# Five convolution taps on ScalarE and adding DMAs, queries and keys turned: one decoder layer on one core

## The chip, the core and the metric

The kernel runs on 1 core of one Trainium2 chip. The metric is the device time of one execution in microseconds (us). The engines are called as the profile calls them: PE (TensorE), DVE (VectorE), ACT (ScalarE), POOL (GpSimd) and SP (SyncE, which issues the loads of the weights).

## What is computed

One decoder layer on 256 tokens of width 1024, all in float32: RMSNorm, one projection to 4608 columns, causal attention of 8 heads beside a convolution module, both gated and merged, an output projection, a residual, a squared-ReLU MLP and a last RMSNorm.

```python
h = rmsnorm(x, g_mix[l])
proj = h @ w_in[l]
q, k, v = the first three blocks of 512 columns, 8 heads of 64
u = proj[..., c_v:c_u] + b_glu[l]
gate_a = jax.nn.sigmoid(proj[..., c_u:c_ga])
gate_c = jax.nn.sigmoid(proj[..., c_ga:])
branch_a = moba_attention(q, k, v) @ w_attn_up[l]      # 256 tokens: plain causal attention
z = a * sigmoid(g)                                      # a, g: the halves of u
z = causal depthwise convolution of z, 31 taps, + b_dw; layernorm; silu
branch_c = z @ w_conv_pw[l] + b_conv_pw[l]
x = x + (gate_a * branch_a + gate_c * branch_c) @ w_out[l]
h = rmsnorm(x, g_ffn[l])
x = x + jnp.square(jax.nn.relu(h @ w_ff1[l])) @ w_ff2[l]
return rmsnorm(x, g_final)
```

## The kernel before, in words

Every float32 product is made of three: each weight and each activation is split into a high part in float32r and the low rest (`w_hi`, `w_lo`, `a_hi`, `a_lo`), and PE sums low by high, high by high and high by low. The weights come in units of 1 MB (512 rows by 512 columns) that SP loads into four slots of `raw`. For each unit n, ACT makes `w_hi` (`high`, L405) and DVE makes `w_lo` (`low`, L674), both three units ahead of PE; the order of work on each engine is written out by hand as one loop over n, with blocks that run at a given n.

Block b is units 2b and 2b+1. Blocks 0 and 1 are the input of the GLU, block 2 the queries (Q), 3 the keys (K), 4 the values (V), 5 to 8 the gates (GA is 5, GC is 7). Units 18 and 19 are the attention's projection, 20 and 21 the convolution's, 22 to 25 the output projection, and the rest is the MLP. A usual unit (`unit`, L980) holds tokens as the stationary operand and streams the weights in 512 columns: 24 matmuls into two PSUM banks, tokens on the partitions. ACT copies a finished block out and scales each token by its `rstd` (`take`, L448). The queries are computed turned (`queries`, L1111): weights stationary, tokens streamed in 256 columns, 48 matmuls a unit, channels on the partitions. The keys are computed as a usual block, copied to `nat`, transposed by PE after unit 8 (L1150, `S_KT`) and copied to `qk_t` (L471). The scores after units 9 to 12 (`scores`, L1067) need `k_made` and `q_made`; each pair of heads then passes over DVE (`row_max`), ACT (`exps`, `normalise`), PE (`probs_transposed`), ACT (`probs_out`) and PE (`values`). Queries keep no `rstd` in `qk_t`; it comes in as the scale of the exponential.

The convolution runs channels on the partitions: `z` holds the input with 30 columns of padding. ACT makes tap 0 with the bias (L539), and DVE adds the other 30 taps for 4 groups of channels, 120 instructions of 256 columns (L730, `conv_products`), spread over the steps by `CONV_AT` and put behind `low` in each step, except in step 15 (`S_OLO`), where the taps come ahead of `low(18)` and of the subtraction that makes `b_lo` (L871). After unit 16 (`S_LN`) PE waits for the last tap (L1168) and transposes `conv` for the LayerNorm; DVE then takes the statistics (L784).

```python
                if n == S_OLO:
                    conv_products(n)
                if n and n + AHEAD < U_LOOP + AHEAD_LOOP:
                    low(n + AHEAD)
```

Of the kernel before, what the change touches and what calls it, by code (L numbers as in the profile page):

```python
# [6 lines left out]
P = 128  # L7
T = 256
# [40 lines left out]
S_QSCALE, S_KT = 6, 8  # L49
# [3 lines left out]
S_GATE = 14  # L53
S_LN = 16
# [5 lines left out]
CONV += [(tap, c) for tap in range(10, TAPS) for c in range(4)]  # L60
CONV_AT = {2: 6, 3: 12, 4: 9, 5: 9, 6: 9, 7: 7, 8: 6, 9: 5, 10: 8, 11: 11, 12: 12, 13: 11, 14: 10, 15: 5}
assert len(CONV) == sum(CONV_AT.values()) == (TAPS - 1) * 4

# [25 lines left out]
def build(nc, x, g_mix, w_in, b_glu, w_dw, b_dw, ln_g, ln_b, w_conv_pw, b_conv_pw,  # L89
# [35 lines left out]
    with ExitStack() as ctx:  # L125
# [12 lines left out]
        a_hi = sb("a_hi", [P, KD, T], F32R)  # L138
        a_lo = sb("a_lo", [P, KD, T], F32R)
# [5 lines left out]
        v_nat = sb("v_nat", [P, TT, A])  # L145
        qk_t = sb("qk_t", [P, 2, CC, T])
# [33 lines left out]
        bias_bc = gfin_bc  # L180
        hid = nat[:, 0, :].rearrange("p (c t) -> p c t", c=4)
# [66 lines left out]
        conv_step = sem("conv_step")  # L248
        conv_tr = sem("conv_tr")
# [7 lines left out]
        cz_lo = sem("cz_lo")  # L257
        q_made = sem("q_made")
        q_scaled = sem("q_scaled")
        k_tr = sem("k_tr")  # L260
# [105 lines left out]
        def _(pool):  # L366
# [21 lines left out]

            inverse_root(1, ln_var[:], 2)
# [3 lines left out]
        def _(act):  # L393
# [47 lines left out]
            def queries_out():  # L441

                act.wait_ge(used, 2 * Q + 2)
                for half in range(2):
                    bank = Q_BANKS[2 * half]
                    nc.scalar.copy(qk_t[:, 0, 2 * half:2 * half + 2], ps[:, bank:bank + 2, 0:T]).then_inc(q_made, 1)

            def take(b):  # L448
# [59 lines left out]

            def set_bias(col):
# [6 lines left out]
            for n in range(U_LOOP):  # L516
# [43 lines left out]
                if n == S_GATE:  # L560
                    act.wait_ge(evac, GA)
# [108 lines left out]
        def _(dve):  # L670
# [76 lines left out]

            def inverse(p):
# [10 lines left out]
            for n in range(U_LOOP):  # L759
# [52 lines left out]
                if n in (U_ATTN, U_ATTN + 1):  # L812
# [3 lines left out]
                    dve.wait_ge(evac, len(ORDER) - 1)  # L816
# [39 lines left out]
                if n == U_FF:  # L856
# [3 lines left out]
                    nc.vector.reciprocal(rsq[:], ms[:, 1]).then_inc(rsq_made, 1)  # L860
                if n == S_OLO:
# [94 lines left out]
        def _(pe):  # L956
# [355 lines left out]
```

## Time and profile before

| | us |
|---|---|
| median of 3 runs | 351.67 |
| lowest and highest run | 351.25, 351.74 |
| span of the profiled execution | 350.3 |
| PE busy | 344.2 (98%) |
| DVE busy | 251.5 (72%) |
| ACT busy | 192.1 (55%) |
| PE's granted clock, mean | 0.997 |

The span runs from the first to the last instruction; the median lies 1.4 us above it. A row of a timeline gives the start, the time from start to end, and how many like instructions were merged. Neighbouring instructions overlap at their ends, so what one costs in a stream is the distance between starts. Line numbers are those of the kernel before.

### The profile page before, as it was taken

To read this page: it belongs to the slowest core of one execution; us is meant where nothing else is said; L and a number is where in the kernel's file an instruction comes from. 1 tells how busy PE (TensorE), PEld (TensorE's weight loads), DVE (VectorE), ACT (ScalarE), POOL (GpSimd) and SP (SyncE) were. 2 spreads that over 40 slices of the span, in tenths; PEclk is the share of its full clock that TensorE was granted. 3 is DMA by queue.
4 is the path that set the end of the run, shared out by engine and by line. 5 is a ranking of instruction groups with operands and counts; after the bars stand their busy time and mean duration, and the time that the engine had idled before them with its cause. 6 is when DMAs were issued, how large, how long until landed. Compare 5 with 4: busy or idle time off the path is not lost.

```text
span 350.3 us, 4670 instructions
## 1 busy us (share of the span) xinstructions
PE 344.2 (98%) x1766; PEld 289.5 (83%) x1766; DVE 251.5 (72%) x313; ACT 192.1 (55%) x236; POOL 3.5 (1%) x13
## 2 busy tenths in 40 slices
PE   8999999999999999999999999999999999999994
PEld 5889988787778888888888888888888888889884
DVE  2969999899999889965666946639466394563813
ACT  4985644698796358434674535515355163551534
POOL 1000000000000000000000000000000000000000
PEclk9999999999999999999999999999999999999998
DMA  8999455534353365783647472944729537260003
GB/s 278 349 387 377 155 206 156 206 122 153 121 198 130 120 239 156 265 254 110 198 157 227 152 252 90 299 180 128 248 102 301 178 121 243 115 239 0 0 0 120
DMA packets 34429, 64.23 MB, mean 183 GB/s; under 512 B 1360, under 2 KB 6000, under 8 KB 34416
## 3 DMA queue, kind: packets, MB, share of 16 engines
q1 hardware_dynamic: 34056, 63.56, 54.0%
q10 hardware_dynamic: 360, 0.49, 0.4%
q8 instruction: 9, 0.15, 0.2%
q14 instruction: 4, 0.03, 0.0%
HBM read 63.00 MB, written 1.05 MB: 183 GB/s over the span
## 4 chain that ended last, share of the span: by engine, by line
PE 98%; DVE 0%; issue 0%; DVEq 0%; ACT 0%
PE ps L971 20%; PE ps L972 19%; PE ps L973 19%; PE ps L1230 17%; PE ps L1238 9%; PE ps L958 4%; PE ps L1018 2%; PE ps L1122 1%; PE ps L1121 1%; PE ps L1123 1%; PE ps L1029 1%; PE ps L1072 1%; PE ps L1097 1%; PE ps L998 1%; PE ps L1191 0%; PE ps L1282 0%
## 5 line engine op out<-in xcount | busy, mean ns | idle before, releaser
L971 PE MATMUL ps<-w_hi,a_lo 128*128 128x512 f32 x256 | 100.9, 394 | 0.0
L972 PE MATMUL ps<-w_hi,a_hi 128*128 128x512 f32 x256 | 99.8, 390 | 0.0
L973 PE MATMUL ps<-w_lo,a_hi 128*128 128x512 f32 x256 | 99.7, 390 | 0.0
L899 DVE TENSOR_TENSOR w_lo<-raw,w_hi 128x2048 fp32r<-128x2048 f32 x28 | 63.5, 2287 | 6.2 <-ACT w_hi L623 6.2
L405 ACT CAST w_hi<-raw 128x2048 fp32r<-128x2048 f32 (+1 forms) x30 | 53.7, 1799 | 19.9 <-PE ps L973 19.7
L1230 PE MATMUL ps<-b_both,w_hi 128*128 128x512 f32 x256 | 61.3, 390 | 0.0
L674 DVE TENSOR_TENSOR w_lo<-raw,w_hi 128x2048 fp32r<-128x2048 f32 x26 | 59.3, 2285 | 1.7 <-ACT w_hi L405 1.7
L623 ACT CAST w_hi<-raw 128x2048 fp32r<-128x2048 f32 x28 | 52.8, 1914 | 7.5 <-PE ps L973 7.5
L971 PEld LDWEIGHTS ps<-w_hi,a_lo 128*128 128x128 f32 x256 | 48.1, 188 | 10.1 <-issue 0.5
L973 PEld LDWEIGHTS ps<-w_lo,a_hi 128*128 128x128 f32 x256 | 48.0, 188 | 10.2
L972 PEld LDWEIGHTS ps<-w_hi,a_hi 128*128 128x128 f32 x256 | 48.1, 188 | 9.4
L1230 PEld LDWEIGHTS ps<-b_both,w_hi 128*128 128x128 f32 x256 | 47.3, 188 | 9.4
L730 DVE SCALAR_TENSOR_TENSOR conv<-z,dw,conv 128x256 f32<-128x256 f32 x120 | 48.5, 478 | 0.0
L878 DVE TENSOR_TENSOR nat<-ps,nat 128x512 f32<-128x512 f32 x16 | 11.1, 692 | 40.6 <-ACT nat L601 40.6
L601 ACT COPY nat<-ps 128x512 f32<-128x512 f32 x16 | 9.4, 587 | 52.9 <-PE ps L1238 52.8
L1238 PEld LDWEIGHTS ps<-b_both,w_lo 128*128 128x128 f32 x256 | 33.0, 191 | 1.3
L1238 PE MATMUL ps<-b_both,w_lo 128*128 128x256 f32 x256 | 33.4, 283 | 0.0
L607 ACT CAST a_hi<-nat 128x1024 fp32r<-128x1024 f32 x7 | 7.3, 1050 | 21.8 <-PE ps L973 21.6
L891 DVE TENSOR_TENSOR a_lo<-nat,a_hi 128x1024 fp32r<-128x1024 f32 x7 | 8.6, 1225 | 14.1 <-ACT a_hi L607 14.1
L971 PE MATMUL ps<-w_hi,b_both 128*128 128x512 f32 x44 | 17.3, 393 | 0.0
L973 PE MATMUL ps<-w_lo,b_both 128*128 128x512 f32 x44 | 17.1, 389 | 0.0
L972 PE MATMUL ps<-w_hi,b_both 128*128 128x512 f32 x44 | 17.1, 389 | 0.0
(138 smaller groups left out, 302.5 us busy)
## 6 DMA issues: line engine op xcount, KB each, us to landing
raw<-in_w_ff_dram SPq DMA_DIRECT2D x32, 1024.0 KB, 5.4
raw<-in_w_in_dram SPq DMA_DIRECT2D x14, 1024.0 KB, 5.9
raw<-in_w_out_dram SPq DMA_DIRECT2D x4, 1024.0 KB, 5.3
raw<-in_w_in_dram SPq DMA_DIRECT2D x14, 256.0 KB, 5.7
raw<-in_w_attn_up_dram SPq DMA_DIRECT2D x2, 1024.0 KB, 5.2
raw<-in_w_conv_pw_dram SPq DMA_DIRECT2D x2, 1024.0 KB, 5.1
res<-in_x_dram SPq DMA_DIRECT2D x2, 512.0 KB, 3.9
raw<-in_w_in_dram SPq DMA_DIRECT2D x4, 128.0 KB, 4.1
```

Source lines behind the costliest of these rows:

```text
L405: nc.scalar.copy(w_hi[:, n % SLOTS, part], raw[:, n % SLOTS, part]).then_inc(hi_made, 1)
L623: nc.scalar.copy(w_hi[:, slot], raw[:, slot]).then_inc(hi_made, 1)
L674: nc.vector.tensor_tensor(w_lo[:, n % SLOTS], raw[:, n % SLOTS], w_hi[:, n % SLOTS].bitcast(F32), ALU.subtract).then_inc(lo_made, 1)
L730: nc.vector.scalar_tensor_tensor(out=conv[:, c], in0=z[:, c, tap:tap + T], scalar=dw[:, w:w + 1], in1=conv[:, c], op0=ALU.mult, op1=ALU.ad ...
L878: nc.vector.tensor_tensor(hid[:, pair], ps[:, TB + 2 * half:TB + 2 * half + 2, 0:T], hid[:, pair], ALU.add).then_inc(sum_made, 1)
L899: nc.vector.tensor_tensor(w_lo[:, slot], raw[:, slot], w_hi[:, slot].bitcast(F32), ALU.subtract).then_inc(lo_made, 1)
L958: return nc.tensor.transpose(dst, src, ident[0:src.shape[0], 0:src.shape[0]])
L971: nc.tensor.matmul(dst, lo[:, tok], w_hi[:, slot, k], start=start, stop=False, skip_group_check=seeded)
L972: nc.tensor.matmul(dst, hi[:, tok], w_hi[:, slot, k], start=False, stop=False, skip_group_check=seeded)
L973: return nc.tensor.matmul(dst, hi[:, tok], w_lo[:, slot, k], start=False, stop=stop, skip_group_check=seeded)
L1230: nc.tensor.matmul(ps[:, TB + c], w_hi[:, slot, k, cols], b_both[:, kk].rearrange("p a t -> p (a t)"), start=kk == 0, stop=False)
L1238: last = nc.tensor.matmul(ps[:, TB + c, 0:T], w_lo[:, slot, k, cols], b_hi[:, kk], start=False, stop=kk == KD - 1)
```

## The change

The queries' function becomes `turned`, for queries and keys. For each group of 128 channels it first streams both halves of the activations (`a_both`, low and high side by side, 512 columns) under each of four `w_hi`, then `a_hi` alone (256 columns) under four `w_lo`. So the product of the low half lands in columns 256 to 511 of a bank; ACT copies that half to `qk_t` and DVE adds the other (`queries_sum` in step 6, `keys_sum` in step 8). The keys' transposes, their `take` and the copy after them go. Keys must still be scaled per token, which now lies along the columns: PE transposes `rstd` after unit 3 into a row, ACT copies it out, and DVE multiplies the keys by it. Scores and unit 10 wait for both halves of the keys.

Taps 26 to 30 leave DVE. ACT multiplies each in steps 5 to 8 (4 instructions of 256 columns a tap): the first into `conv_part` (the room of `zn`), the others by turns into two halves of `gates[:, 1]`; a DMA issued by POOL adds each of these four to `conv_part`, one after the other. In step 16 DVE waits for the last DMA and adds `conv_part` to `conv` in one instruction; PE's transposes wait for that.

```diff
-S_QSCALE, S_KT = 6, 8
+S_QSCALE, S_QSUM, S_KSUM = 6, 6, 8
+K_BANKS = (2, 3, 6, 7)
+S_ROW = 3
...
 S_GATE = 14
+S_PART = 16
...
-CONV += [(tap, c) for tap in range(10, TAPS) for c in range(4)]
-CONV_AT = {2: 6, 3: 12, 4: 9, 5: 9, 6: 9, 7: 7, 8: 6, 9: 5, 10: 8, 11: 11, 12: 12, 13: 11, 14: 10, 15: 5}
-assert len(CONV) == sum(CONV_AT.values()) == (TAPS - 1) * 4
+TAPS_ACT = {5: (26,), 6: (27,), 7: (28, 29), 8: (30,)}
+TAPS_DVE = TAPS - sum(len(taps) for taps in TAPS_ACT.values())
+CONV += [(tap, c) for tap in range(10, TAPS_DVE) for c in range(4)]
+CONV_AT = {2: 6, 3: 12, 4: 9, 5: 9, 6: 6, 7: 7, 8: 2, 9: 3, 10: 6, 11: 9, 12: 10, 13: 9, 14: 7, 15: 5}
+assert len(CONV) == sum(CONV_AT.values()) == (TAPS_DVE - 1) * 4
...
-        a_hi = sb("a_hi", [P, KD, T], F32R)
-        a_lo = sb("a_lo", [P, KD, T], F32R)
+        a_both = sb("a_both", [P, KD, 2, T], F32R)
+        a_hi, a_lo = a_both[:, :, 0], a_both[:, :, 1]
...
+        rstd_row = sb("rstd_row", [P, T])
...
+        tap_out = (gates[:, 1, 0].rearrange("p (c t) -> p c t", c=CC), gates[:, 1, 1].rearrange("p (c t) -> p c t", c=CC))
+        conv_part = zn[:].rearrange("p t c -> p (t c)").rearrange("p (c t) -> p c t", c=CC)
...
+            pool.wait_ge(part_first, CC)
+            for i in range(1, TAPS - TAPS_DVE):
+                pool.wait_ge(tap_made, CC * i)
+                if i > 1:
+                    pool.wait_ge(tap_added, 16 * (i - 1))
+                nc.gpsimd.dma_start(conv_part, tap_out[i % 2], accum_op=ALU.add).then_inc(tap_added, 16)
...
-                    nc.scalar.copy(qk_t[:, 0, 2 * half:2 * half + 2], ps[:, bank:bank + 2, 0:T]).then_inc(q_made, 1)
+                    nc.scalar.copy(qk_t[:, 0, 2 * half:2 * half + 2], ps[:, bank:bank + 2, T:2 * T]).then_inc(q_cross, 1)
...
@@ -451,12 +474,12 @@
                 act.wait_ge(used, 2 * b + 2)
                 if b == 0:
                     act.wait_ge(rstd_made, 1)
-                if b == K:
-                    act.wait_ge(glu_tr, CC)
+                if b == GC:
+                    act.wait_ge(tap_added, 16 * (TAPS - TAPS_DVE - 1))
                 if b == GA:
                     dst, fn = gates[:, 0, :, 0:W], ACT.Copy
-                elif b < 2 or b == K:
-                    dst, fn = nat[:, :, (b % 2) * W:(b % 2) * W + W], ACT.Copy
+                elif b < 2:
+                    dst, fn = nat[:, :, b * W:b * W + W], ACT.Copy
...
             def keys_out():
-                act.wait_ge(k_tr, 1)
-                nc.scalar.copy(qk_t[:, 1], chunks(SB0)).then_inc(k_made, 1)
+
+                act.wait_ge(used, 2 * K + 2)
+                for half in range(2):
+                    bank = K_BANKS[2 * half]
+                    nc.scalar.copy(qk_t[:, 1, 2 * half:2 * half + 2], ps[:, bank:bank + 2, T:2 * T]).then_inc(k_cross, 1)
...
+                for tap in TAPS_ACT.get(step, ()):
+                    act.wait_ge(z_made, CC)
+                    i = tap - TAPS_DVE
+                    if i > 2:
+                        act.wait_ge(tap_added, 16 * (i - 2))
+                    for c in range(CC):
+                        w = tap * CC + c
+                        dst = tap_out[i % 2][:, c] if i else conv_part[:, c]
+                        nc.scalar.activation(dst, z[:, c, tap:tap + T], ACT.Copy,
+                                             scale=dw[:, w:w + 1]).then_inc(tap_made if i else part_first, 1)
...
-                if n == S_KT:
+                tap_products(n)
+                if n == S_ROW:
+                    act.wait_ge(row_tr, 1)
+                    nc.scalar.copy(rstd_row[:], ps[:, SB0, 0:T]).then_inc(row_made, 1)
+                if n == 2 * K + 1:
                     keys_out()
-                if n == 2 * Q + 1:
+                elif n == 2 * Q + 1:
                     queries_out()
                 elif n < U_ATTN and n % 2 == 1 and 0 < n // 2 < GA:
                     take(n // 2)
...
-                    act.wait_ge(evac, GA)
+                    act.wait_ge(evac, GA - 1)
...
+                for half in range(2):
+                    bank = Q_BANKS[2 * half]
+                    dve.wait_ge(q_cross, half + 1)
+                    part = qk_t[:, 0, 2 * half:2 * half + 2]
+                    nc.vector.tensor_tensor(part, ps[:, bank:bank + 2, 0:T], part, ALU.add).then_inc(q_made, 1)
+
+            def keys_sum():
+
+                dve.wait_ge(row_made, 1)
+                row = rstd_row[:].rearrange("p (c t) -> p c t", c=1).to_broadcast([P, 2, T])
+                for half in range(2):
+                    bank = K_BANKS[2 * half]
+                    dve.wait_ge(k_cross, half + 1)
+                    part = qk_t[:, 1, 2 * half:2 * half + 2]
+                    nc.vector.tensor_tensor(part, ps[:, bank:bank + 2, 0:T], part, ALU.add).then_inc(k_sum, 1)
+                for half in range(2):
+                    dve.wait_ge(k_sum, half + 1)
+                    part = qk_t[:, 1, 2 * half:2 * half + 2]
+                    nc.vector.tensor_tensor(part, part, row, ALU.mult).then_inc(k_made, 1)
...
+                if n == S_PART:
+                    dve.wait_ge(tap_added, 16 * (TAPS - TAPS_DVE - 1))
+                    dve.wait_ge(conv_step, (TAPS_DVE - 1) * CC)
+                    nc.vector.tensor_tensor(conv[:], conv[:], conv_part, ALU.add).then_inc(conv_made, 1)
...
-                    dve.wait_ge(evac, len(ORDER) - 1)
+                    dve.wait_ge(evac, len(ORDER) - 2)
...
+                if n == S_QSUM:
+                    queries_sum()
+                if n == S_KSUM:
+                    keys_sum()
...
+                if hb == 1:
+                    pe.wait_ge(row_made, 1)
...
-            def queries(n):
+            def turned(n, banks):
 
                 weights(n)
                 for c in range(CC):
                     if n == 2 * Q and c == 2:
                         pe.wait_ge(z_made, 2)
+                    if n == 2 * K and c == 2:
+                        pe.wait_ge(z_made, CC)
                     cols = slice(c * P, c * P + P)
                     for k in range(HK):
                         kk = HK * (n % 2) + k
-                        dst = ps[:, Q_BANKS[c], 0:T]
-                        nc.tensor.matmul(dst, w_hi[:, n % SLOTS, k, cols], a_lo[:, kk], start=kk == 0, stop=False)
-                        nc.tensor.matmul(dst, w_hi[:, n % SLOTS, k, cols], a_hi[:, kk], start=False, stop=False)
-                        last = nc.tensor.matmul(dst, w_lo[:, n % SLOTS, k, cols], a_hi[:, kk], start=False,
-                                                stop=kk == KD - 1)
+                        nc.tensor.matmul(ps[:, banks[c]], w_hi[:, n % SLOTS, k, cols],
+                                         a_both[:, kk].rearrange("p a t -> p (a t)"), start=kk == 0, stop=False)
+                    for k in range(HK):
+                        kk = HK * (n % 2) + k
+                        last = nc.tensor.matmul(ps[:, banks[c], 0:T], w_lo[:, n % SLOTS, k, cols], a_hi[:, kk],
+                                                start=False, stop=kk == KD - 1)
                     if n == 2 * Q and c == 1:
                         glu_transposed(GLU_AT[n])
                 last.then_inc(used, 1)
...
-                if half == 0 and b >= 2:
-                    pe.wait_ge(evac, b - 1 if b <= V - 1 else b - 2)
+                if half == 0 and b in (Q, K):
+                    pe.wait_ge(evac, b - 1)
+                if n == 2 * GA:
+                    pe.wait_ge(k_made, 2)
+                if half == 0 and b > GA:
+                    pe.wait_ge(evac, b - 3)
                 if n == 2 * V:
                     pe.wait_ge(q_made, 2)
...
-                if b == Q:
-                    queries(n)
+                if b in (Q, K):
+                    turned(n, Q_BANKS if b == Q else K_BANKS)
...
-                if n == S_KT:
-                    pe.wait_ge(evac, K)
-                    pe.wait_ge(z_made, CC)
-                    transpose_chunks(SB0, lambda t, c: nat[:, t, W + c * P:W + c * P + P]).then_inc(k_tr, 1)
+                if n == S_ROW:
+                    pe.wait_ge(rstd_made, 1)
+                    pe.wait_ge(vec_made, 1)
+                    for t in range(TT):
+                        last = transpose(ps[:, SB0, t * P:t * P + P], rstd[:, 0, t:t + 1].to_broadcast([P, P]))
+                    last.then_inc(row_tr, 1)
                 if n == S_ATT:
-                    pe.wait_ge(k_made, 1)
+                    pe.wait_ge(k_made, 2)
...
                 if n == S_ATT + 2:
-                    pe.wait_ge(evac, V)
...
-                    pe.wait_ge(conv_step, (TAPS - 1) * CC)
+                    pe.wait_ge(conv_made, 1)
...
-                pe.wait_ge(evac, len(ORDER) - 2 + col)
+                pe.wait_ge(evac, len(ORDER) - 3 + col)
```

## Rows read from the trace of the kernel before

**Rows 1.** The page: busy time of each engine; the chain that ended last, by engine

```profile
PE 344.2 (98%) x1766; PEld 289.5 (83%) x1766; DVE 251.5 (72%) x313; ACT 192.1 (55%) x236; POOL 3.5 (1%) x13
PE 98%; DVE 0%; issue 0%; DVEq 0%; ACT 0%
```

**Rows 2.** Who waited for whom, PE: in total, times, longest, us

```profile
PE ps L998 <- DVE zero_b L677: 1.2, 1, 1.2
```

**Rows 3.** Timeline of PE, units 4 to 9: start us, us, engine, line, operation

```profile
30.78 0.28 PE L1121 MATMUL ps<-a_lo,w_hi 128*128 128x256 f32 x1
...
33.65 1.03 PE L958 MATMUL ps<-ident,nat 128*128 128x128 f32 x8
...
43.15 0.40 PE L971 MATMUL ps<-w_hi,a_lo 128*128 128x512 f32 x1
...
59.51 1.03 PE L958 MATMUL ps<-ident,nat 128*128 128x128 f32 x8
60.30 0.48 PE L971 MATMUL ps<-w_hi,a_lo 128*128 128x512 f32 x1
...
65.92 0.92 PE L1072 MATMUL ps<-qk_t 64*128 64x256 f32 x8
```

**Rows 4.** Timeline of PE, the first products of the MLP

```profile
177.34 2.00 PE L1230 MATMUL ps<-b_both,w_hi 128*128 128x512 f32 x8
179.18 1.12 PE L1238 MATMUL ps<-b_both,w_lo 128*128 128x256 f32 x8
180.13 3.82 PE L1230 MATMUL ps<-b_both,w_hi 128*128 128x512 f32 x16
```

**Rows 5.** Timeline of DVE from step 8 up to the LayerNorm

```profile
61.39 2.29 DVE L674 TENSOR_TENSOR w_lo<-raw,w_hi 128x2048 fp32r<-128x2048 f32 x1
...
66.95 0.70 DVE L738 TENSOR_TENSOR ps<-ps,mask 128x512 f32<-128x512 f32 x1 [0.89 <-issue]
...
89.67 0.69 DVE L738 TENSOR_TENSOR ps<-ps,mask 128x512 f32<-128x512 f32 x1
...
93.86 4.81 DVE L730 SCALAR_TENSOR_TENSOR conv<-z,dw,conv 128x256 f32<-128x256 f32 x12
...
107.35 6.02 DVE L730 SCALAR_TENSOR_TENSOR conv<-z,dw,conv 128x256 f32<-128x256 f32 x15
113.29 2.28 DVE L674 TENSOR_TENSOR w_lo<-raw,w_hi 128x2048 fp32r<-128x2048 f32 x1
115.50 1.21 DVE L871 TENSOR_TENSOR b_both<-o_t,b_both 128x1024 fp32r<-128x1024 f32 x1
116.63 1.29 DVE L784 BATCH_NORM_STATS2 stats<-ps 128x6 f32<-128x512 f32 x2
```

**Rows 6.** Timeline of DVE, two products of 512 columns out of PSUM

```profile
130.59 1.28 DVE L819 TENSOR_TENSOR nat<-ps,gates 128x512 f32<-128x512 f32 x2
```

**Rows 7.** Timeline of ACT, steps 7 to 13

```profile
54.26 1.27 ACT L466 ACTIVATE nat<-ps,rstd 128x512 f32<-128x512 f32 x2 [3.47 <-PE ps L973]
...
71.27 0.91 ACT L491 ACTIVATE probs<-probs,rinv 128x256 f32<-128x256 f32 x2 [0.24 <-DVE rinv L750]
72.08 0.68 ACT L494 ACTIVATE probs<-probs,rinv 128x128 f32<-128x128 f32 x2
...
91.66 0.57 ACT L477 ACTIVATE probs<-ps,nbias,q_scale 128x256 f32<-128x256 f32 x1 [0.57 <-DVE nbias L746]
...
96.53 1.90 ACT L405 CAST w_hi<-raw 128x2048 fp32r<-128x2048 f32 x1
```

**Rows 8.** Timeline of PE, the last scores and the transposes of conv

```profile
88.52 0.92 PE L1072 MATMUL ps<-qk_t 64*128 64x256 f32 x8
...
114.68 1.03 PE L958 MATMUL ps<-ident,conv 128*128 128x128 f32 x8
```

**Rows 9.** DMA issues by size: KB each, median us from issue to landing

```profile
res<-in_x_dram SPq DMA_DIRECT2D x2, 512.0 KB, 3.9
...
gfin_bc<-in_b_conv_pw_dram SPq DMA_DIRECT2D x1, 512.0 KB, 8.1
```

More of the change, by code:

```diff
@@ L248, in build @@
         conv_step = sem("conv_step")
+        part_first = sem("part_first")
+        tap_made = sem("tap_made")
+        tap_added = sem("tap_added")
+        conv_made = sem("conv_made")
         conv_tr = sem("conv_tr")
@@ L257, in build @@
         cz_lo = sem("cz_lo")
+        q_cross = sem("q_cross")
         q_made = sem("q_made")
         q_scaled = sem("q_scaled")
-        k_tr = sem("k_tr")
+        row_tr = sem("row_tr")
+        row_made = sem("row_made")
+        k_cross = sem("k_cross")
+        k_sum = sem("k_sum")
         k_made = sem("k_made")
@@ L507, in probs_out, with tap_products @@
                 nc.scalar.copy(probs_t[:], ps[:, TB:TB + 2, :].rearrange("p b n -> p (b n)")[:, 0:768]).then_inc(pt_made, 1)
+            def tap_products(step):
+                for tap in TAPS_ACT.get(step, ()):
[8 more added lines that the diff above has]
+                                             scale=dw[:, w:w + 1]).then_inc(tap_made if i else part_first, 1)
             def set_bias(col):
@@ L746, in row_max, with queries_sum @@
                 nc.vector.tensor_tensor(nbias[:, p], smax[:, p], q_neg[:], ALU.mult).then_inc(nbias_made, 1)
+            def queries_sum():
+                for half in range(2):
[15 more added lines that the diff above has]
+                    nc.vector.tensor_tensor(part, part, row, ALU.mult).then_inc(k_made, 1)
             def inverse(p):
@@ L1146, in _ @@
                     transpose(ps[:, SB0 + 1, P:P + TAPS * CC], dw_rows).then_inc(dw_tr, 1)
-                if n == S_KT:
-                    pe.wait_ge(evac, K)
-                    pe.wait_ge(z_made, CC)
-                    transpose_chunks(SB0, lambda t, c: nat[:, t, W + c * P:W + c * P + P]).then_inc(k_tr, 1)
+                if n == S_ROW:
[4 more added lines that the diff above has]
+                    last.then_inc(row_tr, 1)
                 if n == S_ATT:
-                    pe.wait_ge(k_made, 1)
+                    pe.wait_ge(k_made, 2)
                     pe.wait_ge(q_made, 2)
                 if n == S_ATT + 2:
-                    pe.wait_ge(evac, V)
+                    pe.wait_ge(evac, V - 1)
                 if n == S_ATT + PAIRS - 1:
```

## The prediction

> **What bounds the kernel.** I read the page first: PE is busy for 98% of the span, and the chain that ended last is PE throughout [rows 1]. Then the waits of PE: the only one is 1.2 us, before its first instruction [rows 2]. So PE never waits for data once it has begun, and DVE and ACT matter only where they come late for it. Two questions follow: what does the change do to the length of PE's own stream, and does one of the new waits of PE end later than PE arrives? For the second I laid the timelines of DVE, ACT and PE side by side between 30 and 117 us. DVE is nearly without a gap there: it is behind PE, and catches up only where the next thing it needs isn't ready. The sum is made against the span of 350.3 us, and the difference is put on the median of 351.67 us.
>
> **PE's own stream.** *Queries.* Units 4 and 5 run from 30.78 to 43.15 with eight transposes between them [rows 3]. Eight transposes cost 59.51 to 60.30 and a slower restart of 0.09 (unit 9 behind them takes 5.62 us, 60.30 to 65.92, of which 0.08 is the like change to the scores), 0.88 us together. So a unit of 48 matmuls costs (12.37 - 0.88) / 2 = 5.74 us. A usual unit costs (59.51 - 43.15) / 3 = 5.45 us [rows 3]. The columns streamed are the same in all forms, 12,288 a unit; only the cost per instruction differs.
> The new form has its like in the MLP [rows 4]: 8 matmuls of 512 columns take 179.18 - 177.34 = 1.84 us, and 8 of 256 take 0.95 us. At the usual unit's 0.227 a matmul the first would be 1.82, so each change from narrow to wide costs about 0.02 us. `turned` has four groups of 4 wide and 4 narrow: 4 x (0.91 + 0.02 + 0.475) = 5.63 us a unit; with a dearer change (0.04) 5.7, and with none 5.55. I take 5.64.
> Queries: 2 x (5.64 - 5.74) = -0.2 us. Keys: 2 x (5.64 - 5.45) = +0.4 us. *The keys' transposes* go: -0.88. *The transposes of rstd* come: two at 0.1 and a restart of 0.09, +0.3. Sum: -0.2 + 0.4 - 0.9 + 0.3 = -0.4 us, between -0.7 and -0.2. Where nothing waits, this would be all that the change is worth: the taps that DVE loses cost PE nothing before.
>
> **New waits of PE that are met.** The row: `rstd` is long made when unit 3 ends; ACT copies it while PE is in unit 4, ahead of the transposes at 33.65 by more than 1 us: nothing. The queries' banks: ACT copies the half at about 43.5, and DVE adds in step 6, at about 50.7 (two steps before 61.39), two instructions of 0.6 (1.28 for two with the tail [rows 6]); unit 8 asks at 54.9. The keys: unit 7 ends at 43.15 + 2 x 5.45 = 54.05, + 0.6 (row, queries and keys so far); ACT copies two pairs, about 1 us, in place of the `take` at 54.26 [rows 7]. DVE comes to step 8 at 61.4 as before [rows 5], since in step 6 the sums (1.2) replace three taps (1.2). Its four instructions of 512 columns cost 2.4 us; keys are ready at 63.9, and the scores ask at 65.92 - 0.4 = 65.5 [rows 3]. Met, by 1.6 us. Step 8 has 4 taps fewer (1.6 us), so DVE reaches the first `row_max` at 66.9, where before, after an idle 0.89 us, it began at 66.95 behind the scores [rows 5]: the first exponentials begin as before. The first normalisation ends at 72.76 [rows 7], and PE wants it 0.85 us of scores after unit 10, at 73.32 - 0.4 = 72.9. Met by 0.1 to 0.2 us; if PE gains 0.7 it waits here for the rest.
>
> **ACT and the adding DMAs.** Twenty products at 0.41 to 0.5 us (two of 256 columns in SBUF take 0.91 with the tail [rows 7]) are 8 to 10 us; 1.2 us of copies go. In steps 5 to 8 ACT stands idle some 15 us, the 3.47 us ahead of 54.26 among them [rows 7], so the products fit. What is queued behind them: `high` of the next step and the copies of keys and V. The trace has no adding DMA. The bounds of one of 512 KB are the nearest rows of that size, 3.9 and 8.1 us [rows 9]; it reads two sources, so I take 5.5. A tap of step 6 is multiplied at about 48.1; added by 53.6, it lets tap 29 begin 0.8 us late; the second DMA ends at 59.1 and tap 30, `high(12)` (1.9) and then V (wanted at 65.6) follow in time. The condition for no loss is two DMAs in 62.1 - 48.1 = 14 us, 7 us each. The loads of the weights are half of the DMA engines' time and land long before ACT wants them, so they pay nothing.
> Here a rule of the Trainium skill speaks against the change, in DMA: Bandwidth & Descriptors, "Anatomy of one DMA — SWDGE (gpsimd) path": a DMA issued by GpSimd costs about 2.0 us and its bytes at 436 GB/s. By it 512 KB would be 3.2 us (an estimate from that page), and with the second read that Collectives: The Full Stack, "The bandwidth ceiling", describes for the inline add, 4.4 us; no run shown so far has such a DMA.
>
> **The wait that is not met: the sum before the LayerNorm.** Before, the last tap ended at 113.3 [rows 5] and PE asked at 114.68 [rows 8]: 1.4 us to spare. Now DVE makes its last tap, then `low(18)`, then `b_lo`, and only then the add of `conv_part`; these are 2.2 + 1.1 + 1.2 us (113.29, 115.50, 116.63; the add has the shape of `b_lo`, both operands in SBUF) = 4.5 us behind the last tap [rows 5]. What DVE gains before it: 20 taps at 5.94 / 15 = 0.396 us are 7.9 us, less 1.2 and 2.4 for the sums: 4.3 us. That would leave PE just served. But part of the gain goes into waits, for DVE now runs ahead of what feeds it. Forward from the last scores:
> They start at 88.52 - 0.4 and take 0.92 [rows 8]: `row_max(3)` starts at 89.1, not 89.67; DVE, with six taps fewer in steps 9 to 11, is free 0.5 us earlier and waits. From it to the taps of step 12 it is 93.86 - 89.67 = 4.2 us: 93.3. Ten taps: 97.2. `low(16)` needs `high(16)`, which ACT makes after the last exponentials; these start 0.6 us earlier than 91.66, so `high(16)` ends at 96.53 + 1.90 - 0.6 = 97.8 [rows 7]. DVE waits 0.6 us more. Then `low(16)` 2.2, nine taps 3.6, `low(17)` 2.2, twelve taps 4.75: 110.6. Then 2.2 + 1.1 + 1.2 = 115.1. PE arrives at 114.68 - 0.4 = 114.3 and starts, after a wake-up of under 0.1, at 115.2, 0.5 us later than before. It waits 0.8 to 0.9 us.
> Afterwards nothing gives this back. PE is bound again, and the LayerNorm, the zn transposes and the SiLU hang on PE's transposes, so they shift with it; DVE takes its statistics at 116.3, when before it came only at 116.63.
>
> **Forecast.** +0.5 us: 351.67 + 0.5 = 352.2. Its own range is -0.1 to +1.3 (DVE 0.6 us earlier or 0.8 later over 25 us of dense work): 351.6 to 353.0.
>
> **Rivals.** *A, PE is served* (faster side): DVE loses none of its gain in the two waits, ends the add by 114.3, and the whole is PE's own stream, -0.4: 351.3; with the best figures, -0.7, 351.0. For it: 4.3 gained and 1.4 to spare against 4.5 needed. Against it: `high(16)` stands in front. *B, the adding DMAs are slow* (slower side): at 8.1 us each the second ends at 64.3. Tap 30 (1.65) and `high(12)` (1.9) put V at 67.9, the copy, and the table load of the exponential end at 70.4, 1.45 us later than before; PE waits 1.2 us for the first normalisation, `high(16)` comes later by about as much, and the wait at the sum stays: +1.7, 353.4. At 10 us each it is about +5. It decides from 7 us. *C, the sum is dearer or DVE is later*: the add waits for DVE alone, so every 0.1 us in the taps of steps 12 to 15 is 0.1 us of time; two reads of SBUF beside DMAs that write might cost 1 us: +1.3, 353.0.
> B has a second way in: POOL could be held off by a DVE that has hardly a gap. Each DMA would then start up to one subtraction (2.3 us [rows 5]) late, 5.5 + 2.3 = 7.8 us, so about +1.5, 353.2; I give it 0.03 of B's chance. Against it stands the pace of the subtraction, 2048 columns in 2.2 us [rows 5], one column in 1.08 ns, with no sign of a fast form. The Trainium skill, SBUF — State Buffer, "Who interferes with whom", has such a rule: a VectorE instruction in a two-port mode locks GpSimd out while it writes descriptors. By that rule a plain subtraction would not hold POOL up, and no run shown so far has a DMA issued by POOL.
>
> **Chances.** Forecast 0.55, A 0.2, B 0.13, C 0.12. What can be told from no change is 0.2%, 0.7 us. Of the forecast some 0.37 lies within 0.7 us and 0.18 above; of A 0.12 is within and 0.08 is faster; B and half of C are slower. Together: faster 0.1, same 0.53, slower 0.37. The range from 351.1 to 353.6 leaves out the best of A and the worst of B.
>
> **What would show it.** In the profile after: a wait of PE at the transposes of `conv` of 0.8 us, released by DVE's add, and no other above 0.2; unit pairs 4, 5 and 6, 7 at 11.3 us without transposes; DVE waiting 0.4 to 0.7 us for `high(16)` and about 0.5 for the last scores; adding DMAs of 5 to 6 us. Wrong would be: adds over 7 us each with ACT waiting in steps 7 and 8 (B), or no wait of PE at all (A).

## The result and the profile after

The changed kernel takes 352.27 us (median of 16 runs, 351.93 to 353.03) against 351.71 us of the kernel before (also 16 runs): a ratio of 1.0019, 95% interval 1.0011 to 1.0026. One of the 16 executions of the kernel before took 579.18 us, which moves its median by nothing that can be seen here. The forecast was 352.2. The changed kernel is 0.6 us slower, inside the 0.7 us that were called no change.

The page of the changed kernel, busy time and the chain that ended last:

```profile
PE 343.3 (98%) x1744; PEld 287.3 (82%) x1744; DVE 248.7 (71%) x300; ACT 199.1 (57%) x256; POOL 7.1 (2%) x17
PE 88%; DVE 8%; ACT 2%; issue 1%; DVEq 0%
```

Against [rows 1], PE has 22 instructions and 0.9 us of work less, DVE 2.8 us less, ACT 7.0 more. The line to look at is the second: the chain was 98% PE before, and now 8% of it lies on DVE. Somewhere PE has begun to wait. The waits of PE, where [rows 2] had one:

```profile
PE ps L1071 <- DVE zero_b L720: 1.2, 1, 1.2
PE ps L1031 <- DVE conv L848: 0.8, 1, 0.8
PE ps L1031 <- ACT probs L520: 0.5, 1, 0.5
```

The second is the wait at the sum ahead of the LayerNorm (L848 is the sum of `conv_part`), the third the one behind the first normalisation. The wait at the sum in the timeline of PE, against [rows 8]:

```profile
113.79 0.39 PE L1046 MATMUL ps<-w_lo,a_both 128*128 128x512 f32 x1
114.99 1.09 PE L1031 MATMUL ps<-ident,conv 128*128 128x128 f32 x8 [0.81 <-DVE conv L848]
```

The transposes of `conv` start at 114.99 us, 0.31 later than before; the span is 0.3 us longer (350.6 for 350.3). So all of the difference between the two profiled executions is there by the LayerNorm, and nothing is added or given back after it. The medians differ by 0.6, because the profiled execution of before was a slow one. The device time lies some 1.8 us above the span in all of these kernels; the median span of the kernel before is 349.85 us over 28 executions (those beside e1 to e4 below), that of the changed kernel 350.45 over its 16. So the difference of the spans is 0.6 as well, and the profiled 350.3 is 0.45 above what is usual for the kernel before. The chain of the changed kernel in order of time runs back from that wait (start us, us, what):

```profile
89.60 0.69 DVE smax L784
...
90.65 0.16 DVE nbias L789
...
95.82 1.81 ACT w_hi L428
...
97.65 2.29 DVE w_lo L717
99.94 3.56 DVE conv L773 x9
103.51 2.20 DVE w_lo L717
105.71 4.75 DVE conv L773 x12
110.47 0.59 DVE w_lo L717
...
112.58 1.22 DVE b_both L944
113.80 1.15 DVE conv L848
...
114.99 1.09 PE ps L1031 x8
```

It goes from DVE's last maximum, which waits for PE's last scores, over the exponentials and a gate on ACT to `high(16)`, then `low(16)`, nine taps, `low(17)`, twelve taps, `low(18)`, `b_lo` and the sum. That is the path that the prediction walked, step for step. DVE's own waits on the way, in its timeline:

```profile
79.92 0.70 DVE L781 TENSOR_TENSOR ps<-ps,mask 128x512 f32<-128x512 f32 x1 [0.28 <-PE ps L1145]
...
84.62 0.18 DVE L815 RECIPROCAL rinv<-psums 128x4 f32<-128x4 f32 x1 [0.54 <-ACT probs L506]
...
88.86 0.70 DVE L781 TENSOR_TENSOR ps<-ps,mask 128x512 f32<-128x512 f32 x1 [0.53 <-PE ps L1145]
...
97.65 2.29 DVE L717 TENSOR_TENSOR w_lo<-raw,w_hi 128x2048 fp32r<-128x2048 f32 x1 [0.57 <-ACT w_hi L428]
```

Here a part of the gain of the 20 taps went: DVE runs ahead, and then stands 0.3 to 0.6 us until the scores, the exponentials or a high part are there. Between the first maximum and the last tap it waits six times, 2.5 us in all (0.24 and 0.38 us at 74.44 and 77.12 are not shown); before, it waited twice there, 0.6 us in all.

PE's own stream, its timeline from unit 4 to the last scores, against [rows 3] and [rows 8]:

```profile
30.20 0.38 PE L1031 MATMUL ps<-ident,rstd 128*128 128x128 f32 x2
30.34 1.17 PE L1197 MATMUL ps<-a_both,w_hi 128*128 128x512 f32 x4
...
36.89 1.09 PE L1197 MATMUL ps<-a_both,w_hi 128*128 128x512 f32 x4
...
42.50 0.86 PE L1197 MATMUL ps<-a_both,w_hi 128*128 128x512 f32 x3
...
53.73 0.40 PE L1044 MATMUL ps<-w_hi,a_both 128*128 128x512 f32 x1
...
64.75 0.92 PE L1145 MATMUL ps<-qk_t 64*128 64x256 f32 x8
...
71.28 0.92 PE L1145 MATMUL ps<-qk_t 64*128 64x256 f32 x8
72.67 0.87 PE L1031 MATMUL ps<-ident,probs 128*128 128x128 f32 x6 [0.47 <-ACT probs L520]
...
87.89 0.92 PE L1145 MATMUL ps<-qk_t 64*128 64x256 f32 x8
```

Unit 5 is 42.50 - 36.89 = 5.61 us, and units 6 and 7 are 53.73 - 42.50 = 11.23 us. Queries: 12.16 us from 30.34 to 42.50 against 12.37, -0.2; a restart behind the row's transposes, slower by 0.07, is in the 12.16. Keys: 11.23 against 10.90, +0.3. The two transposes of the row take 0.14, +0.1. Units 8 and 9 without the keys' transposes are 11.02 us against 11.87 (54.05 to 65.92), -0.85. Sum: -0.6 us (34.55 us from 30.20 to 64.75, against 35.14 from 30.78 to 65.92). The first scores come 1.17 us earlier than before and not 0.6, because this execution had a head start of 0.58 us: PE's transposes of x, before anything that was changed, took 2.6 us here and 3.1 in the profiled execution of before. The kernels below show the same spread from one execution to the next. DVE has no part in it: its subtraction of step 4 begins at 38.9 us in both.

The head start doesn't reach the end. It is lost at the wait behind the normalisation: from the second scores to the transposes of the probabilities it is 1.39 us (71.28 to 72.67), and 0.85 before (72.47 to 73.32), so this wait costs 0.54 in the stream. The one at the sum costs 0.94: from the last scores to the transposes of `conv` it is 27.10 us (87.89 to 114.99) against 26.16 (88.52 to 114.68). Together -0.58 - 0.59 + 0.54 + 0.94 = +0.31 us, the whole difference.

The adding DMAs on POOL's timeline, and their row among the DMA issues:

```profile
48.05 1.03 POOL L410 DMA_DIRECT2D zn<-gates  x1 [29.08 <-ACT gates L545]
55.32 0.85 POOL L410 DMA_DIRECT2D zn<-gates  x1 [6.23 <-DMA zn<-gates]
62.19 0.84 POOL L410 DMA_DIRECT2D zn<-gates  x1 [6.01 <-DMA zn<-gates]
67.77 0.86 POOL L410 DMA_DIRECT2D zn<-gates  x1 [4.74 <-DMA zn<-gates]
zn<-gates POOLq DMA_DIRECT2D x4, 512.0 KB, 6.5
```

The second of them had landed by 61.74 us, when ACT began the last tap (its timeline is with e6), 13.7 us after the first was issued.

### The profile page after: what moved, and what is told of

Read it like the earlier page. It is cut to its first block, busy times and chain, and to the rows that moved or that the text cites. A ratio compares the mean times of both kernels' runs of the same rounds, so it can differ in the third digit from the quotient of the medians.

```text
span 350.6 us, 4644 instructions
## 1 busy us (share of the span) xinstructions
PE 343.3 (98%) x1744; PEld 287.3 (82%) x1744; DVE 248.7 (71%) x300; ACT 199.1 (57%) x256; POOL 7.1 (2%) x17
## 4 chain that ended last, share of the span: by engine, by line
PE 88%; DVE 8%; ACT 2%; issue 1%; DVEq 0%
PE ps L1314 17%; PE ps L1044 16%; PE ps L1045 16%; PE ps L1046 16%; PE ps L1322 9%; PE ps L1197 4%; DVE w_lo L717 3%; PE ps L1031 3%; DVE conv L773 3%; PE ps L1201 2%; PE ps L1091 2%; PE ps L1102 1%; PE ps L1071 1%; ACT w_hi L428 1%; PE ps L1275 0%
## 5 line engine op out<-in xcount | busy, mean ns | idle before, releaser
L1044 PE MATMUL ps<-w_hi,a_both 128*128 128x512 f32 x240 | 94.6, 394 | 0.0
L1045 PE MATMUL ps<-w_hi,a_both 128*128 128x512 f32 x240 | 93.5, 390 | 0.0
L1046 PE MATMUL ps<-w_lo,a_both 128*128 128x512 f32 x240 | 93.5, 390 | 0.0
L1044 PEld LDWEIGHTS ps<-w_hi,a_both 128*128 128x128 f32 x240 | 45.1, 188 | 9.5 <-issue 0.3
L1046 PEld LDWEIGHTS ps<-w_lo,a_both 128*128 128x128 f32 x240 | 45.0, 188 | 9.6
L1045 PEld LDWEIGHTS ps<-w_hi,a_both 128*128 128x128 f32 x240 | 45.1, 188 | 8.8
L773 DVE SCALAR_TENSOR_TENSOR conv<-z,dw,conv 128x256 f32<-128x256 f32 x100 | 40.6, 478 | 0.0
L650 ACT CAST a_both<-nat 128x1024 fp32r<-128x1024 f32 x7 | 7.3, 1050 | 21.8 <-PE ps L1046 21.6
L964 DVE TENSOR_TENSOR a_both<-nat,a_both 128x1024 fp32r<-128x1024 f32 x7 | 8.6, 1224 | 14.1 <-ACT a_both L650 14.1
L1197 PE MATMUL ps<-a_both,w_hi 128*128 128x512 f32 x64 | 17.6, 397 | 0.0
L1044 PE MATMUL ps<-w_hi,b_both 128*128 128x512 f32 x44 | 17.3, 393 | 0.0
```

Of the source, the lines that this page charges most:

```text
L773: nc.vector.scalar_tensor_tensor(out=conv[:, c], in0=z[:, c, tap:tap + T], scalar=dw[:, w:w + 1], in1=conv[:, c], op0=ALU.mult, op1=ALU.ad ...
L1044: nc.tensor.matmul(dst, lo[:, tok], w_hi[:, slot, k], start=start, stop=False, skip_group_check=seeded)
L1045: nc.tensor.matmul(dst, hi[:, tok], w_hi[:, slot, k], start=False, stop=False, skip_group_check=seeded)
L1046: return nc.tensor.matmul(dst, hi[:, tok], w_lo[:, slot, k], start=False, stop=stop, skip_group_check=seeded)
L1197: nc.tensor.matmul(ps[:, banks[c]], w_hi[:, n % SLOTS, k, cols], a_both[:, kk].rearrange("p a t -> p (a t)"), start=kk == 0, stop=False)
```

## The experiments

The theory, from the prediction: the time is set by DVE's way to the sum of `conv_part`, because 3.4 us of other work stand between the last tap and the sum, and because what DVE gained was lost in its waits. The rivals: PE's own stream costs the 0.6 us; or the adding DMAs do. Ratios are to the kernel before, measured beside each group: 351.68 us for e1 to e4, 351.59 us for e5 to e8.

**The sum earlier (e1).** In step 15 the sum goes right behind the last tap, ahead of `low(18)`.

```diff
-                if n == S_PART:
-                    dve.wait_ge(tap_added, 16 * (TAPS - TAPS_DVE - 1))
-                    dve.wait_ge(conv_step, (TAPS_DVE - 1) * CC)
-                    nc.vector.tensor_tensor(conv[:], conv[:], conv_part, ALU.add).then_inc(conv_made, 1)
...
                 if n == S_OLO:
                     conv_products(n)
+                    dve.wait_ge(tap_added, 16 * (TAPS - TAPS_DVE - 1))
+                    dve.wait_ge(conv_step, (TAPS_DVE - 1) * CC)
+                    nc.vector.tensor_tensor(conv[:], conv[:], conv_part, ALU.add).then_inc(conv_made, 1)
```

> The changed kernel, but DVE makes the sum of conv_part in step 15, right behind its last tap, ahead of low(18) and of b_lo; nothing else moves. Theory T (the wait of 0.8 us at the transposes of conv is DVE's, because 3.4 us of other work stands between the last tap and the sum): the sum ends at 110.4 + 1.2 = 111.6 us, PE asks at 114.1 and doesn't wait there, and the time falls by 0.8 us, to 351.4 to 351.5. Rival R (the 0.6 us come from PE's own stream: the turned units, the row's transposes, the first wait behind the normalisation): the sum's place changes nothing, 352.2 to 352.3.

Measured: 351.30 us, ratio to before 0.9985 (0.9976 to 0.9994), a little better than expected. One instruction moved by two places turns +0.6 into -0.4 us, a step of 0.94 us, which is what the wait cost in PE's stream. The wait at the sum is gone from PE's waits; the one behind the normalisation stays:

```profile
PE ps L1030 <- ACT probs L520: 0.6, 1, 0.6
PE ps L1043 <- DVE w_lo L725: 0.3, 1, 0.3
```

(The second is at 19 us, long before the scores. This profile is of the slowest of e1's 11 executions, 352.62 us, in which DVE was 1.3 us later than usual from the first units on. The wait of 0.5 to 0.6 is in the profile of e2 too, and that execution is a usual one.) PE's own stream isn't what costs.

**Three taps into DVE's waits (e2).** The sum stays where it is; the timetable changes.

```diff
-CONV_AT = {2: 6, 3: 12, 4: 9, 5: 9, 6: 6, 7: 7, 8: 2, 9: 3, 10: 6, 11: 9, 12: 10, 13: 9, 14: 7, 15: 5}
+CONV_AT = {2: 6, 3: 12, 4: 9, 5: 9, 6: 6, 7: 7, 8: 2, 9: 3, 10: 7, 11: 10, 12: 11, 13: 9, 14: 4, 15: 5}
```

> The changed kernel with the sum where it is, but three taps go from step 14 to the steps 10, 11 and 12, one to each (7, 10, 11 and 4 for 6, 9, 10 and 7), where DVE waited 0.3 to 0.6 us for PE and ACT. Theory T (DVE's gain was lost in those waits): the three taps cost nothing where they go and DVE comes to its last tap 3 x 0.4 = 1.2 us earlier, more than the 0.8 us that PE waits: 351.4 to 351.6. If DVE's waits don't matter and only the number of its instructions counts: no change, 352.2 to 352.3.

Measured: 351.27 us, 0.9986 (0.9977 to 0.9995), a little better than expected. DVE does the same instructions as in the changed kernel, and its last wait shrinks from 0.57 to 0.17 us; its waits for the scores are gone. The sum comes early enough (DVE):

```profile
97.59 2.29 DVE L717 TENSOR_TENSOR w_lo<-raw,w_hi 128x2048 fp32r<-128x2048 f32 x1 [0.17 <-ACT w_hi L428]
...
112.48 1.21 DVE L848 TENSOR_TENSOR conv<-conv,zn 128x1024 f32<-128x1024 f32 x1
115.04 1.29 DVE L853 BATCH_NORM_STATS2 stats<-ps 128x6 f32<-128x512 f32 x2 [1.36 <-PE ps L1031]
```

So both halves of the theory hold: the work between tap and sum, and the gain lost in waits, are both needed for the wait of 0.8 us, and mending either one takes it away.

**Each half of the change alone (e3, e4).** e3 has the turned queries and keys with all 30 taps on DVE:

```diff
-TAPS_ACT = {5: (26,), 6: (27,), 7: (28, 29), 8: (30,)}
+TAPS_ACT = {}
-CONV_AT = {2: 6, 3: 12, 4: 9, 5: 9, 6: 6, 7: 7, 8: 2, 9: 3, 10: 6, 11: 9, 12: 10, 13: 9, 14: 7, 15: 5}
+CONV_AT = {2: 6, 3: 12, 4: 9, 5: 9, 6: 6, 7: 7, 8: 2, 9: 5, 10: 8, 11: 11, 12: 13, 13: 12, 14: 12, 15: 8}
...
-                    pe.wait_ge(conv_made, 1)
+                    pe.wait_ge(conv_step, (TAPS_DVE - 1) * CC)
```

> Only the second half of the change: queries and keys turned with their sums on DVE, all 30 taps on DVE again (20 taps more than the changed kernel, put into steps 9 to 15), no products of taps on ACT, no adding DMAs and no sum of conv_part. Theory T: PE's own stream is 0.5 us shorter than before, but DVE has 3.6 us more work than before and comes to its last tap at 115 to 116.5 us instead of 113.4, where PE asks at 114.1: a wait of 1 to 2.3 us, +0.5 to +1.8 against the kernel before, 352.2 to 353.5. If PE's own stream decides: 351.2.

e4 is the kernel before with `TAPS_ACT`, `tap_products`, POOL's loop, the sum in step 16 and the changed kernel's `CONV_AT`; queries and keys are untouched.

> Only the first half of the change: the kernel before (queries as before, keys transposed by PE) with five taps on ACT and the adding DMAs, and the sum in step 16. Theory T: DVE has 7.9 us less work but is held by the scores and by high(16), so it reaches the sum's end at about 115.5 us, where PE asks at 114.7: a wait of 0.8 us and +0.8, 352.5. If the taps that leave DVE were worth time on their own: under 351.7. If the adding DMAs are what costs (ACT waits for them in steps 7 and 8, V comes late): PE waits ahead of the first scores or for the first normalisation, and more than 353.

Measured: e3 353.26 us, 1.0043 (1.0027 to 1.0059); e4 352.48 us, 1.0023 (1.0013 to 1.0032). PE's waits, e3 first, then e4:

```profile
PE ps L1019 <- DVE conv L765: 1.4, 1, 1.4
...
PE ps L1019 <- ACT probs L512: 0.6, 1, 0.6
```

```profile
PE ps L994 <- DVE conv L815: 0.8, 1, 0.8
```

Turned alone, PE's stream is shorter, but DVE's last tap comes 1.4 us after PE asks for it: there is no slack for the sums of queries and keys. The five taps that ACT takes over are thus worth 1.0 us beside the turned keys (353.26 to 352.27), and 2.0 with the early sum (351.30). The taps alone bring the wait at the sum of the changed kernel, at a like 0.8 us, and no wait behind the normalisation; that second wait comes with the keys' sums.

**The taps alone with an early sum (e8).** e4 with the sum moved as in e1.

> e4_taps_alone (the kernel before with five taps on ACT and the adding DMAs, queries and keys as before), with the sum in step 15 ahead of low(18). Theory T: the wait of 0.8 us goes, and as PE's own stream is that of before, so is the time: 351.6 to 351.8. The five taps that leave DVE are worth nothing by themselves. If a lighter DVE were worth time: under 351.4.

Measured: 351.57 us, 0.9995 (0.9986 to 1.0004). Without turned queries and keys, 7.9 us of taps off DVE are worth nothing.

**Both waits (e5).** e1, and the two taps of step 8 go to steps 11 and 12.

```diff
-CONV_AT = {2: 6, 3: 12, 4: 9, 5: 9, 6: 6, 7: 7, 8: 2, 9: 3, 10: 6, 11: 9, 12: 10, 13: 9, 14: 7, 15: 5}
+CONV_AT = {2: 6, 3: 12, 4: 9, 5: 9, 6: 6, 7: 7, 9: 3, 10: 6, 11: 10, 12: 11, 13: 9, 14: 7, 15: 5}
```

> e1_add_early (the sum of conv_part in step 15, ahead of low(18)), and the two taps of step 8 go to the steps 11 and 12 (10 and 11 taps for 9 and 10), so that DVE is free 0.8 us earlier for the first maximum. Theory T2 (the second wait of PE, 0.5 to 0.6 us behind the first normalisation, is there because DVE comes to the first maximum 1.2 us after the scores are there, held by the four sums of the keys and the two taps): that wait goes too, and the time is PE's own stream: e1's 351.3 less 0.5 to 0.6, 350.7 to 350.9. Rival (that wait is ACT's: the table load behind V, which came late for the adding DMAs): it stays, 351.3.

Measured: 351.01 us, 0.9982 (0.9973 to 0.9991). The wait behind the normalisation is gone from PE's waits, and the time is the lowest of all kernels, 0.6 us under before, which is PE's own -0.6. The first maximum starts at 65.90 us, not at 66.81 as in the changed kernel, while PE is at the first scores at 64.87, about as in the changed kernel (64.75). The first maximum on DVE, in the changed kernel and in e5:

```profile
66.81 0.70 DVE L781 TENSOR_TENSOR ps<-ps,mask 128x512 f32<-128x512 f32 x1
...
65.90 0.70 DVE L781 TENSOR_TENSOR ps<-ps,mask 128x512 f32<-128x512 f32 x1
```

PE's transposes of the probabilities follow its second scores without a gap (PE):

```profile
71.41 0.92 PE L1144 MATMUL ps<-qk_t 64*128 64x256 f32 x8
72.26 0.88 PE L1030 MATMUL ps<-ident,probs 128*128 128x128 f32 x6
```

That the wait was DVE's, and not ACT's for its table load, follows from this run. Over e1 it gave 0.1 to 0.3 us (0.1 by the ratios, 0.29 by the medians), with intervals that overlap, less than the 0.5 to 0.6 expected; so the gain in time isn't clear of the noise. The wait follows how long after the start of the first scores DVE begins the first maximum: 2.1 to 2.2 us in the changed kernel, e1, e2 and e3, which wait 0.5 to 0.6; 1.5 in e7, which doesn't, and 1.0 in before, e4, e5 and e8, which don't either. Delay less wait is 1.6 us in all four that wait, so the wait begins at about 1.6.

**Longer adding DMAs (e6).** Each of the four in two halves of 256 KB, one behind the other.

```diff
-                nc.gpsimd.dma_start(conv_part, tap_out[i % 2], accum_op=ALU.add).then_inc(tap_added, 16)
+                for half in range(2):
+                    if i > 1 or half:
+                        pool.wait_ge(tap_added, 32 * (i - 1) + 16 * half)
+                    nc.gpsimd.dma_start(conv_part[:, 2 * half:2 * half + 2], tap_out[i % 2][:, 2 * half:2 * half + 2],
+                                        accum_op=ALU.add).then_inc(tap_added, 16)
```

> The changed kernel with each of the four adding DMAs in two halves of 256 KB, the second issued when the first has landed, so that a tap's addition lasts longer with the same bytes; all else as it was. It measures the price of rival B of the prediction. In the changed kernel one takes 6.5 us and the next is issued 6.9 us after it; if a half takes 4.5 us, a pair takes 9 to 10 and the second pair lands at about 67: tap 30, high(12), V and the table load end at 73 instead of 67.7, and PE waits some 4 us more for the first normalisation, +3 to +4.5 against the changed kernel, 355 to 357. If the adding DMAs have room to spare (the condition of 7 us a DMA is wrong): 352.3.

Measured: 364.42 us, 1.0362 (1.0345 to 1.0379): +12 us, three times what was expected. POOL, ACT and PE of this kernel:

```profile
48.28 1.04 POOL L411 DMA_DIRECT2D zn<-gates  x1 [29.56 <-ACT gates L547]
...
59.98 0.84 POOL L411 DMA_DIRECT2D zn<-gates  x1 [5.46 <-DMA zn<-gates]
...
73.86 1.30 ACT L547 ACTIVATE gates<-z,dw 128x256 f32<-128x256 f32 x3 [9.85 <-DMA zn<-gates]
...
81.96 1.65 PE L1147 MATMUL ps<-qk_t 64*128 64x256 f32 x8 [10.06 <-ACT probs L508]
```

The first pair takes 11.7 us (48.28 to 59.98) and the second 13.9 until ACT goes on at 73.86, not 9 to 10. Tap 30 can begin only at 73.86; `high(12)`, V, the table load and the exponentials queue behind it on ACT, and PE stands for 10.1 us at the second scores. Most of the remaining 2 us is TensorE's clock. PE has no work from 71.9 to 81.96 us. The granted clock is 1.00 until 75 us, 0.50 (the level of 1.2 GHz) between 76 and 85.4, and 1.00 again from 85.7. From the second scores to the third it is 8.88 us (81.96 to 90.84) against 7.13 in the changed kernel without its wait (71.28 to 78.95, less 0.54): 1.7 us. On average over slices of 10 us (columns: PE, PEld, DVE, ACT and POOL busy, then the clock):

```profile
70.00:80.00 10.00, 1.89 (x9) 1.24 (x7) 2.29 (x1) 6.11 (x9) 1.70 (x2) 0.76 0.55 123
80.00:90.00 10.00, 7.96 (x35) 6.61 (x36) 7.29 (x15) 9.51 (x27) 1.70 (x2) 0.72 0.76 182
```

The mechanism of rival B is shown. How far the changed kernel stands from it is in ACT's timeline:

```profile
61.74 1.71 ACT L545 ACTIVATE gates<-z,dw 128x256 f32<-128x256 f32 x4 [2.41 <-DMA zn<-gates]
63.36 1.90 ACT L428 CAST w_hi<-raw 128x2048 fp32r<-128x2048 f32 x1
65.16 1.25 ACT L489 ACTIVATE v_nat<-ps,rstd 128x512 f32<-128x512 f32 x2
66.42 1.28 ACT L503 ACT_TABLE_LOAD   x1
68.80 0.57 ACT L503 ACTIVATE probs<-ps,nbias,q_scale 128x256 f32<-128x256 f32 x1 [1.09 <-DVE nbias L789]
```

From tap 30 on ACT has no gap until the table is loaded; V is copied 0.4 us after PE was done with it, and then ACT waits 1.09 us for DVE. So the first two adding DMAs could be 1.1 us longer together before the exponentials come later. e6 bears this out: tap 30 begins 12.12 us later there (73.86 for 61.74), and the first exponential 11.02 us later (79.82 for 68.80), 1.1 less.

**Four rooms (e7).** The products of the taps get two more rooms in `gates[:, 0]`, and ACT's waits for the DMAs in steps 7 and 8 go. ACT waits for the last DMA ahead of block GA instead of GC, since GA's room is now in use.

```diff
-        tap_out = (gates[:, 1, 0].rearrange("p (c t) -> p c t", c=CC), gates[:, 1, 1].rearrange("p (c t) -> p c t", c=CC))
+        tap_out = [gates[:, g, t].rearrange("p (c t) -> p c t", c=CC) for g in (1, 0) for t in (0, 1)]
...
-                if b == GC:
+                if b == GA:
                     act.wait_ge(tap_added, 16 * (TAPS - TAPS_DVE - 1))
...
-                    if i > 2:
-                        act.wait_ge(tap_added, 16 * (i - 2))
```

> The changed kernel with four rooms for the products instead of two (the halves of gates[:, 0] are the other two), so that ACT never waits for an adding DMA (3.0 and 2.4 us in the changed kernel). Theory T: ACT's waits lie in time that it has to spare, and the time stays at 352.2 to 352.3; PE's two waits of 0.8 and 0.5 us stay. If the waits for the DMAs delay V and the exponentials: 0.3 us or more off.

Measured: 352.15 us, 1.0015 (1.0006 to 1.0025), the same as the changed kernel within the intervals. ACT's 5.4 us of waits for the DMAs cost nothing. The wait of 0.8 us at the sum stays. The one of 0.5 is absent from its profile, against what was expected: in this execution PE reached the scores at 65.36 us, 0.6 later than in the changed kernel's, with DVE where it was, so the late first maximum met a PE that was late itself. Its time is no better for that: PE comes to the transposes of the probabilities at 72.76 us, against 72.67.

**The two waits add up.** The distances between starts on PE, in us, from the profiles; e6 is left out:

| | before | changed | e1 | e2 | e3 | e4 | e5 | e7 | e8 |
|---|---|---|---|---|---|---|---|---|---|
| second scores to transposes of the probabilities | 0.85 | 1.39 | 1.50 | 1.44 | 1.53 | 0.86 | 0.85 | 0.86 | 0.85 |
| from there to the last scores | 15.20 | 15.22 | 15.20 | 15.22 | 15.20 | 15.20 | 15.20 | 15.20 | 15.20 |
| last scores to transposes of `conv` | 26.16 | 27.10 | 26.16 | 26.13 | 27.68 | 27.09 | 26.13 | 27.10 | 26.13 |

The last row is 27.1 us in the changed kernel, e4 and e7 alike, with a wait behind the normalisation or without one. So the wait at the sum doesn't hide what PE lost before it: DVE stands 0.53 us for PE's last scores, and high(16) hangs on the maximum that follows them, so DVE's arrival at the sum moves with PE's. By this, the changed kernel without the two taps in step 8 would be faster by some of the wait, though its sum stayed late; no run tries it.

## Why the prediction was right

- *PE's own stream, -0.4 (-0.7 to -0.2).* Measured -0.6 (-0.59). A turned unit is 5.61 us, 5.64 predicted; the queries are -0.2 and the transposes -0.85 as said, the keys +0.33 for +0.4. The row was put at +0.3; it is 0.14 and the slower restart of 0.07 that is counted with the queries.
- *The wait at the sum, 0.8 to 0.9 us, with the transposes at 115.2.* Measured 0.81 us (0.94 in the stream), at 114.99. DVE's waits on the way were forecast as 0.5 (scores) and 0.6 us (`high(16)`); the rows show 0.53 and 0.57. The sum itself takes 1.22 us for 1.2. e1 and e2 take this wait away from two sides. This is the mechanism of the forecast, and it is shown.
- *Nothing is given back later.* The 0.31 us at the transposes are the 0.3 us of the span.
- *The wait behind the normalisation was called met by 0.1 to 0.2 us.* This was wrong in the profiled execution, which waits 0.47. DVE's arrival at the first maximum was right (66.9, measured 66.81). What failed is PE's arrival: it was taken from the profiled execution of before, whose start was slow, and PE's own stream was taken 0.2 us too long. With a usual start and -0.6, PE comes early enough to wait. e5 shows that DVE's late maximum is the cause. By the medians this wait costs about 0.2 us: e1 and e2, which keep only this one, are 0.4 under before, and e5, which has none, 0.6. Their intervals overlap, so this 0.2 is an estimate.
- *So the number is in part luck.* The forecast was -0.4 + 0.9 + 0; the runs give -0.6 + 0.9 + 0.2. Two misses of 0.2 us cancel. Of the signs named in advance, two came out otherwise: PE has another wait above 0.2 us, and the adding DMAs took 6.5 us and not 5 to 6.
- *The adding DMAs, 5.5 us with a limit of 14 us for two.* Mis-sized: 6.5 us to landing (median). The first two had landed after 13.7 us, so the limit was met by 0.3; by ACT's wait of 1.1 us behind them the true limit was 14.8. Rival B's way of costing time was right: e6 delays the first exponential by just what the DMAs are late beyond that room. The Trainium skill, DMA: Bandwidth & Descriptors, "Anatomy of one DMA — SWDGE (gpsimd) path", gives 3.2 us for these bytes, and 4.4 with the second read that Collectives: The Full Stack, "The bandwidth ceiling", describes (estimates from the pages' figures); the trace has 6.5. Both are below the 5.5 of the prediction, so they speak for the change and not against it, as the prediction has it. In the stretch from 55 to 62 us the DMA engines are busy 99% of the time with these and the weights (the last but one figure of the row), which neither figure counts:

```profile
55.00:62.00 7.00, 7.00 (x33) 5.77 (x32) 7.00 (x13) 4.59 (x8) 0.85 (x1) 1.00 0.99 276
```

- *A (PE is served) and C (a dearer sum)* didn't happen. A is what e1 and e2 make true: 351.3, the time that the prediction gave it. DVE held off by POOL, or POOL by DVE, isn't seen: DVE's subtraction takes 2.29 us beside the DMAs, and 2.29 before. POOL issues the third DMA 0.45 us after the second has landed (62.19 behind 61.74) and takes 0.84 us over it; in e6 it issues one at 74.31, behind a landing at 73.86, while DVE has nothing to do from 69.2 to 77.4 us, and the two times are the same.
- The chances of no change add up to 0.55 (0.37, 0.12 and half of C) where the text has 0.53; nothing hangs on it.

## What to carry to other kernels

Work taken off an engine that is behind isn't time gained until it arrives at the wait that matters. Here 7.9 us of taps off DVE gave nothing alone (e4, e8) and paid only for what the turned keys put on it (e3): part went into waits, and two instructions with a later due time stood between the last tap and the new sum. When a result is split over engines, put the instruction that joins the parts first in its step, ahead of what can wait, and give the freed slots to the steps in which the engine waits. Walk the helper engine's queue forward from its last wait, with distances between starts, and compare its arrival with PE's; in this case that gave a wait of 0.81 us to within 0.1. A helper that itself waits for PE on the way moves with PE, so its wait at the end doesn't hide an earlier one. And before a profiled execution is taken as the base of a sum, compare its span with those of the other executions: here it lay 0.45 us above the median one, nearly as much as the forecast difference.

## What had not been expected of the hardware

- Beside the loads of the weights an adding DMA of half the bytes is not much quicker. From one issue to the next it is 7.3, 6.9 and 5.6 us for 512 KB in the changed kernel, with the DMA engines busy for 86 to 100% of the time; in e6 it is 5.4, 6.3, 6.5 and 7.8 us for the first four of 256 KB, with them busy for 72 to 82%, and 3.5 and 3.9 us for the next two (43% and 58%). So halving them nearly doubles a chain. How much of it is a cost per DMA and how much the sharing with the loads isn't separated by these runs.
- PE's transposes of x took 2.0 to 3.3 us in the profiled executions of these kernels, with the granted clock at full (1.00 in before, the changed kernel, e1 and e7). In e8 the profile names the landing of x as the cause (0.9 us); for the others it wasn't settled.
- In e6 PE had no work from 71.9 to 81.96 us. TensorE's granted clock was 1.00 up to 75 us, 0.50 from 76 us until 85.4, after PE had begun again at 81.96, and 1.00 from 85.7. This cost 1.7 us.
